# A 2-layer decoder step: an earlier start of the memory keys, the last pack of experts spread by halves, and three products put into a routing stage

## The reference

```python
for i in range(DEPTH):                                   # memory of the prompt
    kv = rmsnorm(mem_prompt, mem_norm[i]) @ w_mem_kv[i]
    mk.append(kv[..., :XA_WIDTH]); mv.append(kv[..., XA_WIDTH:])
...
    h = rmsnorm(x, norm_mix[i])
    z = h @ w_in                                         # conv_w_in or ret_w_in
    mix, ns = conv_mixer(...) or retention_mixer(...)
    xa = cross_attn(q_x, mem_ks[i], mem_vs[i])
    x = x + concatenate([mix, xa]) @ w_out
    x = x + hier_moe(rmsnorm(x, norm_ffn[i]), w_group, w_router, w_gate_up, w_down)
return rmsnorm(x, final_norm), ...                       # and keys, values, states
```

## Time and profile before

| | us |
|---|---|
| median of 3 runs | 1252.75 (1252.19 to 1254.45) |
| the profiled execution, its own time | 1249.18 |
| span of its trace | 1247.4 |
| PE busy | 1172.2 |
| memory, keys and values of layer 0 | 0 to 75 |
| routing and experts of layer 0 | 307 to 565 |
| retention, attention, projection of layer 1 | 565 to 1012 |
| routing and experts of layer 1 | 1012 to 1232 |
| last norm and stores | 1232 to 1247.4 |

### The profile page before, as it was taken

One profiled execution on the slowest core, in us unless ns is written; L12 is line 12 of the kernel. 1 busy time (PEld: TensorE's weight loads), 2 busy tenths in 40 slices (PEclk: granted clock), 3 DMA queues, 4 the chain that ended last, 5 costly groups with the idle time before them and its releaser, 6 DMA issues.

```text
span 1247.4 us, 13730 instructions
## 1 busy us (share of the span) xinstructions
PE 1172.2 (94%) x5940; PEld 692.4 (56%) x5940; DVE 349.1 (28%) x851; ACT 155.3 (12%) x365; POOL 12.8 (1%) x24
## 2 busy tenths in 40 slices
PE   6999999999999998979999999999999989998875
PEld 5667776677544342436655656566677753432333
DVE  3221113211213231336224242424300022422224
ACT  2000002111211110111201011011200031100002
POOL 0000000000000000000000000000000000000000
PEclk9999999999999999999999999999999989998898
DMA  9843336833599999999234657383985379999992
GB/s 394 367 176 136 135 139 283 366 147 108 233 428 418 428 428 428 427 427 427 107 135 185 244 192 289 135 353 130 412 349 194 135 280 429 393 428 427 428 427 125
DMA packets 27727, 364.59 MB, mean 292 GB/s; under 512 B 3232, under 2 KB 3248, under 8 KB 4624
## 3 DMA queue, kind: packets, MB, share of 16 engines
q1 hardware_dynamic: 24624, 338.99, 66.5%
q10 hardware_dynamic: 1568, 18.88, 3.6%
q0 software_dynamic: 1472, 5.81, 1.2%
HBM read 339.34 MB, written 24.32 MB: 292 GB/s over the span
## 4 chain that ended last, share of the span: by engine, by line
PE 83%; DMA 13%; DVE 2%; issue 1%; ACT 1%; POOL 0%; SPq 0%; DVEq 0%; POOLq 0%
PE bank L718 23%; PE bank L474 13%; DMA ring<-in_gu 11%; PE bank L577 6%; PE bank L555 5%; PE bank L379 5%; PE bank L798 4%; PE bank L384 4%; PE bank L609 3%; PE bank L587 3%; DMA ring<-in_dn 2%; PE bank L769 1%; PE bank L430 1%; PE bank L363 1%; PE bank L879 1%; PE bank L397 1%
## 5 line engine op out<-in xcount | busy, mean ns | idle before, releaser
L718 PE MATMUL bank<-hT,ring 128*128 128x288 f32 x1088 | 268.2, 407 | 0.8 <-issue 0.8
L718 PEld LDWEIGHTS bank<-hT,ring 128*128 128x128 f32 x1088 | 205.7, 190 | 66.8 <-issue 11.8
L474 PE MATMUL bank<-arena,ring 128*128 128x288 f32 x640 | 158.5, 407 | 1.8 <-DVEq L1241 1.8
L577 PE MATMUL bank<-ring,arena 128*32 128x512 f32 x944 | 115.5, 630 | 28.8 <-DMA ring<-in_gu 28.8
L474 PEld LDWEIGHTS bank<-arena,ring 128*128 128x128 f32 x640 | 120.2, 190 | 34.2 <-issue 2.2
L555 PE MATMUL bank<-arena 128*128 128x512 f32 (+1 forms) x192 | 98.5, 640 | 1.1 <-DVE arena L1316 1.1
L577 PEld LDWEIGHTS bank<-ring,arena 128*32 128x32 f32 x944 | 30.3, 113 | 107.0 <-issue 81.2
L609 PE MATMUL bank<-arena 128*128 128x288 f32 x256 | 68.6, 412 | 2.1 <-issue 1.7
L555 PEld LDWEIGHTS bank<-arena 128*128 128x128 f32 (+1 forms) x192 | 32.2, 193 | 66.7 <-issue 65.4
L1333 DVE TENSOR_TENSOR xT<-xT,bank 128x288 f32<-128x288 f32 x128 | 58.1, 454 | 10.2 <-PE bank L609 6.3
L379 PE MATMUL bank<-arena,ring 128*128 128x256 f32 x256 | 57.9, 388 | 3.1 <-DVE arena L1180 3.1
(11 more groups left out here) (233 smaller groups left out, 845.7 us busy)
## 6 DMA issues: line engine op xcount, KB each, us to landing
ring<-in_gu SPq DMA_DIRECT2D x59, 2048.0 KB, 22.1
ring<-in_dn SPq DMA_DIRECT2D x32, 2048.0 KB, 20.0
ring<-in_rin SPq DMA_DIRECT2D x14, 2048.0 KB, 12.4
ring<-in_wkv SPq DMA_DIRECT2D x8, 2048.0 KB, 20.2
ring<-in_cin SPq DMA_DIRECT2D x8, 2048.0 KB, 16.7
ring<-in_kc SPq DMA_DIRECT2D x8, 2048.0 KB, 7.8
ring<-in_vc SPq DMA_DIRECT2D x8, 2048.0 KB, 10.5
ring<-in_st SPq DMA_DIRECT2D x8, 2048.0 KB, 10.3
```

The costliest lines, as they stand in the source:

```text
L474: mm = pe.matmul(bank[1 + o % 4][:, 0:T], w[:, k, :], cat[:, k, :], start=(k == 0), stop=(k == kt - 1))
L577: mm = pe.matmul(bank[2][32 * e:32 * e + 32, :], xt[:, k, 32 * e:32 * e + 32], wv[e // 2][:, e % 2, kk, :], start=(k == 0), stop=(k == KD ...
L718: mm = pe.matmul(outs[o], w[:, o, k, :], src[:, k, :], start=(k == 0), stop=(k == KD - 1))
```

## The change

In the order of the program:

- The eps column moves from `cst` to `par`. SP issues `par` first, then `memT` in two halves, then the first half of key chunk 0 with a semaphore of its own (`first_keys`), then `cst`, then the other half of the chunk, then xT and the ring as before. The key weights are laid out so that one half of a chunk holds all that one piece needs.
- DVE first writes `hmu`, memory times gain without the per-token factor. PE makes key pieces 0 and 1 from `hmu`, with the sum of squares (now collected by DVE, so 2 products in place of 8) between them. DVE multiplies these two pieces by the factor as it takes them out of PSUM (`keys_scaled`, 2 instructions of 128x512); ACT takes out pieces 2 and 3 alone.
- In both layers, the spread of pack 6 moves ahead of the last gate-up chunk of pack 7, and goes to banks 0, 1, 4. The spread of pack 7 is done in two halves, each after its half of the down projection.
- In layer 1, squares of the final norm go to `hT` as each tile is added, DVE collects the first four, and PE's sums (`final_sums`) stand beside the spread: one product after the down projection and four at the end.
- In layer 1's routing, PE does two products of identity by decay (128x512, into bank 3, read by nobody) before the wait for the choice, and one after the ranks.
- y is stored in three pieces: tiles 0 to 3 and 6 to 7 by SP, tiles 4 to 5 by ACT.

```diff
@@ SP
-            sp.dma_start(memT, a["memT"]).then_inc(S("mem_in"), 16)
+            sp.dma_start(par[:, :], a["par"]).then_inc(S("par_in"), 16)
+            for q in range(2):
+                sp.dma_start(memT[:, 4 * q:4 * q + 4, :], a["memT"][:, 4 * q:4 * q + 4, :]).then_inc(S(f"mem_in{q}"), 16)
+            half = SLOT // 2
+            sp.dma_start(slot(0)[:, 0:half], a["wkv"][0][:, 0:half]).then_inc(S("first_keys"), 16)
             sp.dma_start(cst[:, :], a["cst"]).then_inc(S("const_in"), 16)
-            sp.dma_start(par[:, :], a["par"]).then_inc(S("const_in"), 16)
...
+            for k0, k1 in ((0, 4), (6, 8)):
+                sp.wait_ge(S("normed"), NORM_DONE["final"] - KD + k1)
+                sp.dma_start(a["out_y"][:, k0:k1], hT[:, k0:k1]).then_inc(S("y_stored"), 16)
@@ PE, start
-            pe.wait_ge(S("const_in"), 32)
+            memory_kv(0, 0)
+            pe.wait_ge(S("const_in"), 16)
             norm_sum("mem", NM)
+            memory_kv(0, 1)
             pe.wait_ge(S("ms_out"), 1)
-            for j in range(4):
+            for j in (2, 3):
                 memory_kv(0, j)
@@ PE, routing
                 if i == 0:
                     memory_kv(1, 0)
+                else:
+                    for _ in range(FILL):
+                        pe.matmul(bank[3][:, :], C("ident"), C("decay")[:, 0:512], start=True, stop=True)
                 pe.wait_ge(S("htok_out"), KD * (i + 1))
                 pe.wait_ge(S("chosen"), i + 1)
...
                 if i == 0:
                     memory_kv(1, 1)
+                else:
+                    pe.matmul(bank[3][:, :], C("ident"), C("decay")[:, 0:512], start=True, stop=True)
@@ PE, experts
+                        if c == 3 and i == PACKS - 1:
+                            combine(i - 1)
                         gate_up_chunk(c, gate_up_landed(L, i, c), xgT).then_inc(S("gu_sum"), 1)
...
-                    if i:
+                    if i and i < PACKS - 1:
                         combine(i - 1)
...
                         down_half(n, landed(pe, ("dn", (L, i, n)))).then_inc(S("y_sum"), 1)
-                combine(PACKS - 1)
+                        if i == PACKS - 1 and L == 1 and n == 1:
+                            pe.wait_ge(S("squares_added"), 5)
+                            final_sums((0,), "squared", KD * NORM["final"])
+                        if i == PACKS - 1:
+                            combine(i, range(4 * n, 4 * n + 4))
+                        if i == PACKS - 1 and L == 1 and n == 1:
+                            final_sums(range(4, KD), "squared", KD * NORM["final"]).then_inc(S("final_sum"), 1)
@@ DVE, start
+            for k in range(KD):
+                dve.wait_ge(S(f"mem_in{k // 4}"), 16)
+                dve.tensor_scalar(hmu[:, k, :], memT[:, k, :], G("mem0")[:, k:k + 1], None, ALU.mult) \
+                   .then_inc(S("gained"), 1)
+            for k in range(KD):
+                add_square("mem", NM, k)
             norm("mem", memT, ((hm0, "mem0"), (hm1, "mem1")), NM)
+            for j in range(2):
+                dve.wait_ge(S("kv_sum"), j + 1)
+                dve.tensor_tensor(KT[:, 2 * j:2 * j + 2, :], v3(bank[j][:, :], 2),
+                                  rstd[:, 0:NM].unsqueeze(1).to_broadcast([P, 2, NM]), ALU.mult) \
+                   .then_inc(S("keys_scaled"), 1)
```

More of the change, by code:

```diff
@@ L40 @@
 SPILL = 6
+FILL = 2
 CAP = 32
@@ L152, in build @@
         hm0 = v3(ar(CATO + 2048, KD * NM), KD)
+        hmu = v3(ar(CATO + 4096, KD * NM), KD)
         qx = v3(ar(PHO, 8 * T), 8)
@@ L605, in turn_picked, with spread @@
                 return mm
-            def spread(o):
-                return pe.matmul(bank[2 + o % 3][:, 0:T], yo[:, o * P:(o + 1) * P], GT, start=True, stop=True)
+            def spread(o, b):
+                return pe.matmul(bank[b][:, 0:T], yo[:, o * P:(o + 1) * P], GT, start=True, stop=True)
             def experts(L):
@@ L622, in turn_x, with combine @@
                     turn_picked(1, xg).then_inc(S("xg_turned"), 1)
-                def combine(i):
-                    pe.wait_ge(S("y_out_a"), PACKS * L + i + 1)
-                    pe.wait_ge(S("y_out_d"), PACKS * L + i + 1)
+                def combine(i, part=range(KD)):
                     pe.wait_ge(S("gt_out"), PACKS * L + i + 1)
-                    for o in range(KD):
-                        if o == 1:
+                    for o in part:
+                        if o == 0:
+                            pe.wait_ge(S("y_out_a"), PACKS * L + i + 1)
+                        if o == 0 and i:
+                            pe.wait_ge(S("y_added"), KD * PACKS * L + KD * i)
+                        if o == 4:
+                            pe.wait_ge(S("y_out_d"), PACKS * L + i + 1)
+                        if o == 1 and i != PACKS - 2:
                             pe.wait_ge(S("actT_out"), PACKS * L + min(i + 2, PACKS))
@@ L705, in experts, with final_sums @@
                                     pe.wait_ge(S(f"spill_dve{L}"), it * STEP_DVE + (SPILL_DVE["rows_out"] + o - 2))
-                                spread(o).then_inc(S(f"spill_pe{L}"), 1)
+                                spread(o, SPREAD[0][o % 3]).then_inc(S(f"spill_pe{L}"), 1)
                             pe.wait_ge(S(f"spill_dve{L}"), it * STEP_DVE + SPILL_DVE["added"])
+                    if L == 1:
+                        final_sums(range(KD), "spill_squared", 0).then_inc(S("spill_sum"), 1)
+            def final_sums(ks, ready, first):
+                for k in ks:
+                    pe.wait_ge(S(ready), first + k + 1)
+                    mm = pe.matmul(bank[7][:, 0:T], C("ones"), hT[:, k, :], start=(k == 0), stop=(k == KD - 1))
+                return mm
             def project_in(name, c, src, drained):
@@ L1350, in turned_out, with add_pack @@
                     dve.tensor_copy(xgT[:, 4:8, :], v3(bank[1][:, :], 4)).then_inc(S("xt_out_d"), 1)
-                def add_pack(i):
-                    for o in range(KD):
+                def add_pack(i, part=range(KD)):
+                    for o in part:
                         dve.wait_ge(S("spread"), KD * PACKS * L + KD * i + o + 1)
-                        add_rows(o).then_inc(S("y_added"), 1)
+                        add_rows(o, SPREAD[i == PACKS - 2][o % 3]).then_inc(S("y_added"), 1)
                 select(0)
@@ L1383, in experts @@
                         select(i + 2)
+                    if i == PACKS - 1:
+                        add_pack(i, range(4))
+                    if i == PACKS - 1 and L == 1:
+                        for k in range(1, 4):
+                            dve.wait_ge(S("squared"), KD * NORM["final"] + k + 1)
+                            ins = dve.tensor_tensor(hT[:, 0, :], hT[:, 0, :], hT[:, k, :], ALU.add)
+                            if k < 3:
+                                V_(ins)
+                        ins.then_inc(S("squares_added"), 1)
                     dve.wait_ge(S("y_sum"), 2 * PACKS * L + 2 * i + 2)
                     dve.tensor_copy(yo[:, 512:1024], bank[6][:, :]).then_inc(S("y_out_d"), 1)
-                add_pack(PACKS - 1)
+                add_pack(PACKS - 1, range(4, KD))
                 with dve.If(more > 0):
@@ L1636, in _ @@
             experts(1)
-            for q in range(2):
-                ks = slice(4 * q, 4 * q + 4)
-                pool.wait_ge(S("normed"), NORM_DONE["final"] - 4 + 4 * q)
-                pool.dma_start(a["out_y"][:, ks], hT[:, ks]).then_inc(S("y_stored"), 16)
-            pool.wait_ge(S("y_stored"), 32)
+            pool.wait_ge(S("y_stored"), 48)
             pool.wait_ge(S("conv_stored"), 32)
```

94 lines of the change are left out of this document (64 added, 30 removed).

## The result

The changed kernel takes 1237.3 us (median of 4 runs, 1235.74 to 1238.07), the kernel before 1252.47 (4 runs, 1251.39 to 1254.45). The ratio is 0.9878, with an interval of 0.9859 to 0.9896. The medians are 15.2 us apart; 16.8 were forecast. The profiled execution of the change took 1237.39 us with a span of 1235.6, 11.8 less than the span before. The table sets the forecast against the two profiles, stage by stage.

A forecast was written before the change was run, and what follows sets the result against it. Two regimes were taken: PE's chain between plateaus, DMA at 427 to 429 GB/s on the expert plateaus. Gains 7.0 + 2.1 + 1.3 + 6.4 = 16.8 us, from the 1252.75 median, gave 1236.0; range 1231.5 to 1241.

The forecast's parts named there:

- Start, 7.0 forecast: Before the convolution's projection: keys start on an early half chunk and end at 38.8 us against 45.75, gaining 7.0 us.
- one more issue of 0.42 us: At the start: one extra load issue ahead moves the half chunk's landing from about 8.3 to 8.5 us.
- half of 3.1, 1.55 us: First key products: a slow-clock spell of about 3.1 us now falls on them and costs 1.55 us.
- The rival of the half chunk that comes with the rest: At the start: queued loads mix, half chunk lands at 13.8 us, gain only 11.5, time 1241.3; chance 0.07.
- a full clock at the start: Start and routing: first products and fill run at 2.4 GHz, gain 19.3 us, time 1233.4; chance 0.15.
- Layer 0, 2.1 forecast: Layer 0's last pack: moved spreads fall into chunk waits, four products remain after the last down half; gain 2.1 us.
- Routing, 1.3 forecast: Layer 1's routing: fill runs slow and delays the choice about 1 us, picks run fast; gain 1.3 us.
- The choice between the rows: Layer 1's routing: layer 0's busy row at half clock taken as nearest, giving 1.3 us instead of 2.3.
- the 2.3 of the rival: Layer 1's routing: fill at full clock, picks 2.03 us and ranks some 0.3 faster; full-clock rival's chance 0.15.
- That all of the saving reaches the end: Before layer 1's last stream: PE starts that stream at 1068 us, so earlier savings count, up to 2.1 us and a little.
- End, 6.4 forecast: Layer 1's last pack to the last store: sums end 5.8 us earlier, smaller last store saves 0.6; gain 6.4 us.
- The moved spread fills the wait from 1211.5 to 1215.6, and the chunk then takes 1.9 us: Layer 1's last pack: last gate-up chunk runs at full clock after the spread and ends at 1217.5 us.

The follow-up runs named there:

- The warm-up: Six 128x512 products of a constant tile added before the first key product, against the changed kernel: 1233.91 us, ratio 0.9842.
- the start alone: Kernel before with only the change's edits ahead of the first projection (halved loads, unscaled memory, collected squares): 1244.45 us, ratio 0.9932.
- the end alone: Kernel before with only the change's last packs, final sums and stores; start and routing as before: 1245.55 us, ratio 0.9933.

## Why the prediction was right, and where it was not

By its size the forecast holds: 1236.0 predicted, 1237.3 measured, inside 1231.5 to 1241. But its terms hold less well than the total. The start, the fill and the end gained by the mechanisms forecast, and the first and the last gained less; layer 0's gain is not there on average. Most of what was missed is one thing, the slow clock, at the start, in layer 0's last pack and at the end.

**Start, 7.0 forecast, 5.1 measured.** The first key product, forecast for 8.5 us, came at 9.39. The step that gave 8.5 took the landing of the earlier trace rows and added "one more issue of 0.42 us"; it took the rate of the loads as unchanged. The windows show 0.8 us of the 0.9 as a lower rate from 3 to 7 us, of which moving the parameters gave back 0.3. The term "half of 3.1, 1.55 us" for the slow spell should have been 2.6: the spell lasted from 9.4 to at least 13.8 us, which is over 4.4 and not 3.1. The warm-up returned 2.57, so that is shown. Together 0.9 + 1.0 = 1.9, which is the whole miss. The rival of the half chunk that comes with the rest is refuted by 9.35 us against its 13.8; that of a full clock at the start needed the warm-up to come true.

**Layer 0, 2.1 forecast, 1.9 between the two profiles, nothing on average.** From the first gate-up product of layer 0 to the projection of layer 1, three traces without the new last pack have 231.9 to 232.6 us, mean 232.1. Six with it as in the change (the warm-up's among them) have 230.0 to 233.6, mean 232.2. The 1.9 us between the profiles is thus luck. Two things take the gain back. First, the working left out that the spread of pack 6, once moved off the end, stands behind a waited-for chunk, where the clock can fall: from the third chunk to the fourth it is 5.9 us in two of the six traces, 7.6 in one and 8.7 to 8.8 in three. From the third chunk to the projection the six have 22.9 us on average and the three 23.5, so only 0.6 us is left of the 2.1. Second, the third chunk itself comes 0.7 us later after the first product (209.3 on average against 208.6); no run shows why. The slow clock is not peculiar to the move, though: in the start alone, and with the spread put back, it falls on the fourth chunk (3.35 and 3.34 us). Two traces of the same program, the change and its repetition, differ by 1.6 us from the third chunk to the projection (21.2 and 22.8), so which of the cases an execution gets is not set by the program alone.

**Routing, 1.3 forecast, 1.5 between profiles, about 3 on average.** The choice between the rows was right for this profile and most others: the slow spell fell on the fill (3.50 us), as in layer 0, and the picks ran fast. So it is in five of eight traces (3.25 to 3.58 us, routing 15.4). In the other three the fill itself ran at full clock (1.88 us) and the routing took 14.7, which is 2.2 less than before: the 2.3 of the rival. The forecast chose between the two; over the traces both occur. The gain was taken against one execution of the kernel before whose picks took 7.96 us, and that is near the short end of 7.78 to 11.46. The Trainium skill (TensorE: Matmul & The Clock Gate, What's actually happening) lets activity release the gate; in the trace of the end alone PE was busy without a break from 1022 to 1030 us at 0.50, so activity did not release it soon there. That all of the saving reaches the end, and is not hidden by the stream, is confirmed: from the first gate-up product of pack 0 to the third chunk of pack 7 the ten traces in which the spread of pack 6 is not placed still earlier have 181.0 to 182.0 us, though that product starts anywhere from 1019.4 to 1032.1. The stream waits for PE at the dry spot, and passes a shift on. Why it is 181.0 in some and 181.9 in others is open; that is the 0.9 lost between the profiles.

**End, 6.4 forecast, 4.2 measured, 4.15 in each of the six traces with the change's order.** The step that failed is "The moved spread fills the wait from 1211.5 to 1215.6, and the chunk then takes 1.9 us". The fourth chunk did take 1.9 us, but it came late: the third chunk ahead of it took 3.55 us at half clock and not 1.92, so the fourth was used 1.6 us after the time forecast, and the second down half started 1.9 us after its own. The forecast had the half clock of the earlier trace rows go with the wait; it moved to the chunk before, behind a wait of 2.08 us, where before a wait of 3.07 us had left that chunk at full clock. In all six traces third chunk and spread together take 7.6 us up to the fourth chunk, 1.6 more than at full clock, whether the slow spell lies more on the one or on the other (2.40 to 3.55 us for the chunk). Trying to move the spread further showed the bound behind it: the first down chunk is not there before 1212.3. The rest of the path was 0.7 longer than forecast, the steps behind it and the smaller last store 0.3 shorter.

**The total** came within 1.3 us by luck: errors cancel. Between profiles the gain is 11.8, 5 under the forecast. The kernel before, whose runs go from 1248.5 to 1256.7 us, was profiled in a short execution; its median (1252.47) lies 3.3 above, while the change, with a fill that takes the long spells away, has its profile at its median. Taking the savings "from the median" was right for the number, but for a reason the prediction did not have. That the spell in routing makes the difference between long and short executions fits the traces without the fill (4 us between routings of 20.9 and 16.9, in two programs with the same routing code), but no program without the fill was traced both short and long. For the runs without a trace it is argued, with one sign: of the 47 runs of the kernel before in the experiments, the ten below 1249.5 us have a mean granted clock of 0.983 to 0.985, while of the 23 above 1253.2 us 20 have one of 0.975 to 0.981. The other three have the clock of the short ones, so the slow clock is not all of it.

## What to carry to other kernels

After a wait of PE, put down the next few microseconds at both clock levels, and ask on what they will fall. Work moved ahead to fill a wait may come to stand where the clock falls. Products whose result nobody reads, placed while PE waits anyway, took the slow spell on themselves here and narrowed the spread between runs; at a place where PE need not wait they cost their own time (1.98 or 3.33 us here, by the clock). Before a term of one or two microseconds is made from one profile, compare that execution with the median, and the stage with the same one in a second trace.

## What the runs showed that was not expected

- The same routing code took 16.9 us in the kernel before and 20.9 in the kernel with only the end changed, by the length of one spell at 1.2 GHz that lasted up to 20 us with PE busy for most of it. Where one program without the fill was traced twice, the two traces agreed within 0.2 us (16.9 and 16.7, 19.4 and 19.4).
- The slow clock at the start, 338 ns a weight load in place of 190, does not show in the page's clock row, which has 1.00 there.
- Six warming products at the start, before anything has landed, gave 2.3 us in the traces, more than any other edit made on top of the change.
- DMA engines as busy as before moved 233 GB/s in place of 434 from 3 to 4 us when a tile of 97 columns stood first in the queue and the memory came in halves. With that tile issued by ACT it was 206, so its place first in that queue is not the cause.
